# Gated linear attention rewritten by pairs of heads: half-array products, state updates on all partitions, PSUM banks of their own

## What is computed

```python
def gla_blocked(q, k, v, log_a, s0):
    bcum = jnp.cumsum(ac, axis=-2)            # per block of 64 (prompt) or 16 (streams) rows
    b_last = bcum[..., -1:, :]
    q_in, k_in = qc * jnp.exp(bcum), kc * jnp.exp(-bcum)
    att = jnp.where(causal, jnp.einsum('nbhik,nbhjk->nbhij', q_in, k_in), 0.0)
    o_intra = jnp.einsum('nbhij,nbhjv->nbhiv', att, vc)
    k_state = kc * jnp.exp(b_last - bcum)
    def step(s, inp):
        o = jnp.einsum('bhik,bhkv->bhiv', qi, s)
        s = at[..., None] * s + jnp.einsum('bhjk,bhjv->bhkv', ks, vi)
        return s, o
# then: rmsnorm(o, gla_g) * silu(ag)
```

## Time and profile before

| | us |
|---|---|
| median of 3 runs | 2823.79 (2822.34 to 2826.65) |
| the profiled execution, its own time | 2827.22 |
| its span, first to last instruction | 2825.4 |
| TensorE busy | 2717.4 (96%) |
| VectorE busy | 681.3 (24%) |
| ScalarE busy | 688.2 (24%) |
| GpSimd busy | 1054.1 (37%) |
| mean granted clock of TensorE | 0.968 of full speed |

### The profile page before, as it was taken

The page is one execution under the profiler, slowest core; times in us unless marked ns, Lnnn a source line. Parts: engine busy times, 40 slices in busy tenths (PEclk is TensorE's granted clock), DMA queues, the critical chain, the costliest instruction groups (busy, mean ns, idle before and its releaser), DMA issues.

```text
span 2825.4 us, 46758 instructions
## 1 busy us (share of the span) xinstructions
PE 2717.4 (96%) x19779; PEld 2580.6 (91%) x19779; DVE 681.3 (24%) x1442; ACT 688.2 (24%) x913; POOL 1054.1 (37%) x403
## 2 busy tenths in 40 slices
PE   7999999999889999999999999999988899999997
PEld 6999999998758999999999999999944489999997
DVE  4110113343443211112311011231133332110112
ACT  2221222220162221122222122221044532211221
POOL 3443444331043444344444334333223343443442
PEclk9999999998599999999999999999989999999998
DMA  3212211223062221221222222133699932222211
GB/s 134 75 60 85 79 58 63 90 75 128 11 237 104 67 76 63 90 75 59 78 78 68 78 82 70 57 108 97 227 358 372 366 120 75 74 67 82 74 62 65
DMA packets 57248, 302.96 MB, mean 107 GB/s; under 512 B 8337, under 2 KB 12194, under 8 KB 31026
## 3 DMA queue, kind: packets, MB, share of 16 engines
q1 hardware_dynamic: 57138, 301.38, 30.4%
HBM read 279.95 MB, written 21.41 MB: 107 GB/s over the span
## 4 chain that ended last, share of the span: by engine, by line
PE 91%; DMA 5%; DVE 2%; ACT 1%; POOL 1%; issue 0%; SPq 0%; DVEq 0%; ACTq 0%; POOLq 0%
PE ps L312 78%; PE ps L676 4%; DMA kv_ring<-in_fox_kc 2%; DMA kv_ring<-in_fox_vc 2%; PE ps L982 1%; PE ps L1016 1%; PE ps L941 1%; PE ps L956 1%; POOL w_lo L298 1%; PE ps L997 1%; PE ps L967 1%; PE ps L1271 0%; DVE xn_lo L413 0%; PE ps L1260 0%; PE ps L378 0%
## 5 line engine op out<-in xcount | busy, mean ns | idle before, releaser
L298 POOL TENSOR_TENSOR w_lo<-w_raw,w_hi 128x2048 fp32r<-128x2048 f32 (+2 forms) x185 | 791.7, 4280 | 687.6 <-ACT w_hi L293 679.2
L312 PE MATMUL ps<-xn_hi,w_hi 128*128 128x320 f32 x3616 | 830.1, 311 | 23.4 <-POOL w_lo L1649 11.0
L312 PE MATMUL ps<-xn_lo,w_hi 128*128 128x320 f32 x3616 | 827.1, 310 | 0.0
L312 PE MATMUL ps<-xn_hi,w_lo 128*128 128x320 f32 x3616 | 826.3, 310 | 0.0
L312 PEld LDWEIGHTS ps<-xn_hi,w_hi 128*128 128x128 f32 x3616 | 606.8, 189 | 25.8 <-POOL w_lo L1649 11.0
L312 PEld LDWEIGHTS ps<-xn_lo,w_hi 128*128 128x128 f32 x3616 | 607.9, 189 | 0.0
L312 PEld LDWEIGHTS ps<-xn_hi,w_lo 128*128 128x128 f32 x3616 | 607.3, 189 | 0.0
L293 ACT ACTIVATE w_hi<-w_raw 128x2048 fp32r<-128x2048 f32 (+2 forms) x185 | 326.6, 1766 | 535.0 <-PE ps L312 466.8
L565 POOL TENSOR_TENSOR h_lo<-prod,h_hi 128x640 f32 x88 | 139.0, 1580 | 716.2 <-ACT h_hi L518 716.2
L312 PE MATMUL ps<-h_hi,w_lo 128*128 128x320 f32 x1408 | 320.9, 309 | 0.0
L312 PE MATMUL ps<-h_hi,w_hi 128*128 128x320 f32 x1408 | 320.9, 309 | 0.0
(11 more groups left out here) (196 smaller groups left out, 1889.3 us busy)
## 6 DMA issues: line engine op xcount, KB each, us to landing
w_raw<-in_w_up SPq DMA_DIRECT2D x87, 1024.0 KB, 4.8
kv_ring<-in_fox_kc SPq DMA_DIRECT2D x32, 1024.0 KB, 13.1
kv_ring<-in_fox_vc SPq DMA_DIRECT2D x32, 1024.0 KB, 12.6
w_raw<-in_w_down_a SPq DMA_DIRECT2D x32, 768.0 KB, 4.2
w_raw<-in_w_in SPq DMA_DIRECT2D x24, 1024.0 KB, 4.9
w_raw<-in_w_down_b SPq DMA_DIRECT2D x32, 640.0 KB, 3.9
fox_s_s<-s_bias_dram SPq DMA_DIRECT2D x16, 576.0 KB, 9.8
kv_ring<-in_band_kc SPq DMA_DIRECT2D x8, 1024.0 KB, 6.2
```

Of the source, the lines that this page charges most:

```text
L298: nc.gpsimd.tensor_tensor(out=w_lo[:, slot, 0:cols], in0=w_raw[:, slot, 0:cols], in1=w_hi[:, slot, 0:cols].bitcast(F32), op=ALU.subtract). ...
L312: last = nc.tensor.matmul(ps[:, 2 * unit + half, 0:HALF], w_part[:, slot, w:w + P], a_part[:, k, half * HALF:(half + 1) * HALF], start=k = ...
```

## The change

Everything lies within the GLA.

- The two zero-filled copies of the queries are gone: one product of 128 partitions scales `qa`. Attention blocks and state products use the 64 rows of their head, in both operands.
- `head_psum` gives each head two banks of its own; `chunk_kv` each chunk a bank; `pair_att`, `pair_stats` and `stream_kv` place the rest. Products on rows 0-63 and on rows 64-127 that stand next to each other go to different banks. In the attention blocks two tiles share a pair of banks, so the masks wait for both.
- Chunk and stream products are now made by head, 64 columns of the array each, written to the partitions of that head. They hold no unused blocks. VectorE then copies and updates both heads of a pair in one instruction of 128 partitions. Chunk products no longer wait for the states, but (from the third chunk on) for the masks that free their banks.
- `pair_out` makes the outputs of two heads, the heads by turns. Squares have a tile for each head of a pair. The statistics, the inverse root (on ten columns) and the diagonals are made by pairs.
- The stream products come in two runs of four streams, with new places in the order: `pair_out(0)`, `pair_out(1)`, `pair_stat(0)`, two spreads, `pair_stat(1)`, four streams, two spreads, four streams.

```diff
-    qa1 = place("qa1", [P, 2, T], F32, at_e + tile_b)
     k_in = place("k_in", [P, 2, T], F32, at_e + 5 * tile_b)
     assert at_e + 7 * tile_b <= end
-    sq_head = place("sq_head", [P, T], F32, at_e)
+    sq_head = [place(f"sq_head{u}", [P, T], F32, at_e + u * tile_b) for u in range(2)]
...
-            pe.wait_ge(g_qk, 6)
+            pe.wait_ge(g_qk, 3)
...
+    def head_psum(h):
+        return flat((2, 4, 0, 6)[h], 2, T)
+    def pair_stats(pair):
+        return ps[:, (5, 7)[pair], 256:256 + 2 * TT]
+    def chunk_kv(c):
+        return ps[:, c, 0:256].rearrange("p (a v) -> p a v", a=2)
+    def pair_att(tt):
+        c0 = tt % 2 * 256
+        return ps[:, 2:8, c0:c0 + 256].rearrange("p (b r) (a c) -> p b r a c", r=2, a=2)[:, tt // 2, :, :, :]
+    def stream_kv(b):
+        return ps[:, 2 + b // 2, b % 2 * 256:b % 2 * 256 + 256].rearrange("p (a v) -> p a v", a=2)
...
-                last = nc.tensor.matmul(ps[:, 3 + tt, h * P:(h + 1) * P], k_in[:, h // 2, cols],
-                                        q_head[h % 2][:, h // 2, cols], start=True, stop=True)
+                last = nc.tensor.matmul(pair_att(tt)[:, h % 2, h // 2, :], k_in[head_rows[h], h // 2, cols],
+                                        qa[head_rows[h], h // 2, cols], start=True, stop=True)
             last.then_inc(g_att, 1)
         for c in range(SEQ // CHUNK):
             rows = slice(64 * (c % 2), 64 * (c % 2) + 64)
             if c >= 2:
...
+                pe.wait_ge(g_attm, min(c // 2 * 2, TT))
+            for h in range(H_A):
+                last = nc.tensor.matmul(chunk_kv(c)[head_rows[h], h // 2, :],
+                                        k_tok[rows, c // 2, h * DK:(h + 1) * DK],
+                                        va[rows, c // 2, h * P:(h + 1) * P], start=True, stop=True)
             last.then_inc(g_kv, 1)
         pe.wait_ge(g_attm, TT)
-        pe.wait_ge(g_s, 4 * (SEQ // CHUNK))
+        pe.wait_ge(g_s, 2 * (SEQ // CHUNK))
         pe.wait_ge(s_dec_loaded, 16)
...
+        def pair_out(pair):
+            heads = (2 * pair, 2 * pair + 1)
             for tt in range(TT):
-                nc.tensor.matmul(o[:, tt * P:(tt + 1) * P], va[:, tt, h * P:(h + 1) * P],
-                                 att[:, tt, h * P:(h + 1) * P], start=True, stop=False)
+                for h in heads:
+                    nc.tensor.matmul(head_psum(h)[:, tt * P:(tt + 1) * P], va[:, tt, h * P:(h + 1) * P],
+                                     att[:, tt, h * P:(h + 1) * P], start=True, stop=False)
                 if tt < TT - 1:
                     for c in (2 * tt, 2 * tt + 1):
                         if c:
                             cols = slice(c * CHUNK, (c + 1) * CHUNK)
-                            last = nc.tensor.matmul(o[:, cols], s_hist[:, c, pair, :], q[:, pair, cols],
-                                                    start=False, stop=c % 2 == 1)
+                            for h in heads:
+                                nc.tensor.matmul(head_psum(h)[:, cols], s_hist[head_rows[h], c, pair, :],
+                                                 qa[head_rows[h], pair, cols], start=False, stop=c % 2 == 1)
                 else:
                     for b in range(DEC_BATCH):
                         cols = slice(SEQ + b * DEC_SEQ, SEQ + (b + 1) * DEC_SEQ)
-                        last = nc.tensor.matmul(o[:, cols], s_dec[:, b, pair, :], q[:, pair, cols],
-                                                start=False, stop=b == DEC_BATCH - 1)
+                        for h in heads:
+                            last = nc.tensor.matmul(head_psum(h)[:, cols], s_dec[head_rows[h], b, pair, :],
+                                                    qa[head_rows[h], pair, cols], start=False,
+                                                    stop=b == DEC_BATCH - 1)
             last.then_inc(g_o, 1)
-        def head_stat(h):
-            pe.wait_ge(g_sq, h + 1)
+        def pair_stat(pair):
+            pe.wait_ge(g_oc, 2 * pair + 2)
+            for h in (2 * pair, 2 * pair + 1):
+                pe.wait_ge(g_sq, h + 1)
+                for tt in range(TT):
+                    last = nc.tensor.matmul(pair_stats(pair)[:, h % 2 * TT + tt:h % 2 * TT + tt + 1],
+                                            sq_head[h % 2][:, tt * P:(tt + 1) * P], mean_head[:, :], start=True,
+                                            stop=True)
+                last.then_inc(g_stat, 1)
+        def head_spread(h):
+            pe.wait_ge(diag_done, DIAG0["gla"] + TT * (h + 1))
             for tt in range(TT):
...
+                last = nc.tensor.matmul(head_psum(h)[:, tt * P:(tt + 1) * P], ones[:, :], diag_a[:, h % 2, tt, :],
                                         start=True, stop=True)
             last.then_inc(g_r, 1)
...
+        def streams_kv(first):
+            pe.wait_ge(g_kown, 1)
+            for b in range(first, first + 4):
+                for h in range(H_A):
+                    last = nc.tensor.matmul(stream_kv(b)[head_rows[h], h // 2, :], k_own[:, b, h * DK:(h + 1) * DK],
+                                            va[:, TT - 1, h * P:(h + 1) * P], start=True, stop=True)
+                last.then_inc(g_kv, 1)
+        pair_out(0)
+        pair_out(1)
+        pair_stat(0)
         head_spread(0)
-        head_stat(1)
-        head_out(3)
         head_spread(1)
...
+        pair_stat(1)
+        pe.wait_ge(g_on, 2)
+        streams_kv(0)
+        head_spread(2)
         head_spread(3)
+        pe.wait_ge(g_on, 4)
+        streams_kv(4)
...
-        for h in range(H_A):
-            act.wait_ge(g_o, h + 1)
-            if h == 2:
+        for pair in range(2):
+            heads = (2 * pair, 2 * pair + 1)
+            act.wait_ge(g_o, pair + 1)
+            if pair:
                 act.wait_ge(g_kown, 1)
...
+            for h in heads:
+                nc.scalar.activation(o_head[:, h, :], head_psum(h), ACT.Copy).then_inc(g_oc, 1)
+            for h in heads:
+                act.wait_ge(g_oc, h + 1)
+                if pair:
+                    act.wait_ge(g_stat, h - 1)
+                nc.scalar.activation(sq_head[h % 2][:, :], o_head[:, h, :], ACT.Square).then_inc(g_sq, 1)
...
-            nc.vector.tensor_tensor(out=qa1[64:P, :, :], in0=qa[64:P, :, :], in1=e_cum[64:P, :, :],
+            nc.vector.tensor_tensor(out=qa[:, :, :], in0=qa[:, :, :], in1=e_cum[:, :, :],
                                     op=ALU.mult).then_inc(g_qk, 1)
...
         for tt in range(TT):
...
+            dve.wait_ge(g_att, min(tt // 2 * 2 + 2, TT))
+            keep = (keep16 if tt == TT - 1 else keep64)[:, :].unsqueeze(1).unsqueeze(1).broadcast_to([P, 2, 2, P])
+            nc.vector.tensor_tensor(out=att[:, tt, :].rearrange("p (a r c) -> p r a c", a=2, r=2), in0=pair_att(tt),
+                                    in1=keep, op=ALU.mult).then_inc(g_attm, 1)
         for c in range(SEQ // CHUNK):
             dve.wait_ge(g_kv, c + 1)
             if c:
...
+                dve.wait_ge(g_s, 2 * c)
+            for pair in range(2):
+                kv = chunk_kv(c)[:, pair, :]
                 if c == 0:
-                    ins_ = nc.vector.tensor_copy(s_hist[rows, 1, pair, :], kv)
+                    ins_ = nc.vector.tensor_copy(s_hist[:, 1, pair, :], kv)
                 else:
                     col = (c + 1) * CHUNK - 1
-                    ins_ = nc.vector.scalar_tensor_tensor(out=s_hist[rows, c + 1, pair, :],
-                                                          in0=s_hist[rows, c, pair, :],
-                                                          scalar=e_cum[rows, pair, col:col + 1], in1=kv,
+                    ins_ = nc.vector.scalar_tensor_tensor(out=s_hist[:, c + 1, pair, :], in0=s_hist[:, c, pair, :],
+                                                          scalar=e_cum[:, pair, col:col + 1], in1=kv,
                                                           op0=ALU.mult, op1=ALU.add)
                 ins_.then_inc(g_s, 1)
...
...
+        def pair_norm(pair):
+            dve.wait_ge(g_stat, 2 * pair + 2)
+            rs_chain(dve, pair_stats(pair), pair * 2 * TT, 2 * TT, RS_NORM0["gla"] + pair * RS_OPS)
+            dve.wait_ge(rs_step, RS_NORM0["gla"] + (pair + 1) * RS_OPS)
+            if pair:
+                dve.wait_ge(g_r, 2)
+            for h in (2 * pair, 2 * pair + 1):
+                for tt in range(TT):
+                    nc.vector.tensor_scalar(out=diag_a[:, h % 2, tt, :], in0=ident[:, :],
+                                            scalar1=rs[1][:, h * TT + tt:h * TT + tt + 1], scalar2=None,
+                                            op0=ALU.mult).then_inc(diag_done, 1)
         def head_gated(h):
             dve.wait_ge(g_r, h + 1)
...
             else:
                 dve.wait_ge(g_sg, 1)
             nc.vector.scalar_tensor_tensor(out=o_tmp[:, :], in0=o_head[:, h, :], scalar=head_gain[:, 0:1],
```

(13 more changed lines are left out.)

88 lines of the change are left out of this document (4 added, 84 removed).

## The result

The changed kernel takes **2797.28 us** (median; 2795.59 to 2798.28, 4 runs), the kernel before 2825.22 us beside it (2822.34 to 2827.09, 4 runs): ratio 0.9901, 95% interval 0.9889 to 0.9913, so 24.6 to 31.4 us less. The forecast was 2797.5 us, its range 2786 to 2809.

The account below looks back on a forecast made before the run. Bound taken: the GLA stretch before the band attention, by VectorE's state chain, TensorE's per-record pace at low clock, then mutual waits. Attention starts at 752.9 instead of 779.25 us, -26.3 us: 2823.8 - 26.3 = 2797.5 us, range 2786 to 2809.

Parts of the forecast that it names:

- the new wait: GLA tail: TensorE waits 3.3 us for the first diagonals, with the first spread queued behind them.
- Scaled queries (1): Query scaling on VectorE, among projections: one 128-partition product replaces two products and two memsets; worth 0.
- Masks (2): VectorE's five attention-block masks run nearly back to back, ending near 686.0 instead of 686.6 us: -0.6 us.
- Chunk states (3): State chain with 128-partition updates, 0.83 us a chunk: outputs start at 692.6 instead of 700.75 us, -8.1 us.
- Outputs by pairs (4): GLA outputs on TensorE: 12.8 us a pair, 25.6 for both against 34.2 before, ten switches of 0.25 us a pair.
- The tail (5): GLA after the outputs, from 718.2 us: statistics, diagonals, spreads, stream products and gates, last gated product ending at 749.9 us.
- the granted clock stays 0.50 to the attention: Sign expected in the profile after: TensorE's clock stays low through the GLA until the band attention.
- The end (6): Cast, subtraction and state store as before; attention's first product at 752.9 instead of 779.25 us.
- the clock that comes back during the outputs: Rival: clock 1.00 from the second output pair on, 6.7 us for that pair, 14 us more gained, 2783.5 us; chance 14%.
- No overlap: Rival: state products within an output pair don't overlap, +6.0 us a pair, 2809.5 us; chance 9%.
- Attention at the low clock: Rival: band attention behind the GLA never regains its clock, up to 55 us added, some 2850 us; chance 3%.
- nothing gained: Rival: something else, say a transfer, holds the attention behind the GLA; time near 2822 us; chance 4%.

Follow-up runs that it names:

- updates_64_sorted: Changed kernel with VectorE's chunk-state copies and updates head by head on 64 partitions, heads ordered 0, 2, 1, 3: 2803.39 us, ratio 0.9922.
- before_states: Kernel before, plus only chunk products by head in 64 columns and VectorE's state copies and updates over 128 partitions: 2815.49 us, ratio 0.9973.
- outputs_grouped: Changed kernel with each pair's full-array output products all issued before its state products, two changes of shape a pair instead of ten: 2786.14 us, ratio 0.9874.
- heads_in_runs: Changed kernel with, within each tile, the even head's state products all before the odd head's instead of by turns: 2801.98 us, ratio 0.9923.
- stats_between: Changed kernel with the first pair's statistics issued within the second pair's outputs, before its third tile: 2795.31 us, ratio 0.9896.
- pool_held: Changed kernel with GpSimd's four GLA subtractions held until VectorE has made all twenty diagonals: 2794.89 us, ratio 0.989.
- clock_kept: Changed kernel plus five unused float32 products of 512 columns on TensorE during the chunk-state chain: 2791.75 us, ratio 0.9879.
- combined: Changed kernel with grouped outputs started during the state chain, first statistics behind the second pair's full-array products, GpSimd's subtractions held: 2773.67 us, ratio 0.9813.

## Why the prediction was right, point by point

The time came out within 0.3 us of the forecast, but that closeness is partly luck. The stage by itself gained 29.7 us where the sum had 26.3: the outputs started 1.8 us sooner than forecast, took 0.5 us longer, and the tail was 2.2 us shorter. Between the medians the gain was 27.9 us, and the median of before beside it lay 1.4 us above the 2823.8 from which the forecast was taken; the two differences of 1.6 and 1.4 us cancel. The profiled execution, forecast at 2800.9 us, took 2795.59. What was right is the order of the parts, the overlap and the new wait. By the steps, counted in the profiled executions:

- **Scaled queries (1): 0.** Nothing waited for them; the projections' end shows only the variation between runs. It wasn't tried by itself.
- **Masks (2): right.** They end 4.3 us after the first attention block; forecast 686.0 - 681.1 = 4.9, before 5.5. The masks start every 0.62 us, each taking 0.68, as they follow each other without a wait.
- **Chunk states (3): mechanism right, size off.** From masks to outputs 5.5 us, forecast 6.6; the start of the outputs comes 9.9 us sooner, forecast 8.1 (before 700.75 - 681.12 = 19.6, now 9.8). The mis-sized term is "each costs what a 64-partition one does: 1.49 / 4 = 0.37 us". The duration is indeed the same (0.34), but that 0.37 was the pitch of updates that change rows each time; wide ones follow every 0.265 us, and a chunk's boundary adds 0.18. So a chunk takes 0.71 us, below the forecast's 0.83 and outside its bounds of 0.75 and 1.1. `updates_64_sorted` shows it, and `before_states` shows that the wide updates alone carry this step.
- **Outputs by pairs (4): right.** 13.1 and 13.05 us, forecast 12.8 each. Ten switches at 0.25 us stand, by the records of the changed kernel (see `outputs_grouped`); the steps of two take 0.213 instead of 0.20. `heads_in_runs` shows the overlap. So the factor on 34.2 us of outputs is 1.31. The Trainium skill's table of theoretical speedups (TensorEngine Tiling (Array Packing), Theoretical Speedup) gives up to 2x. For the half-array products alone the trace comes near it: the attention blocks fell from 4.73 to 2.50 us at full clock, a pair's stream products from 2 x 3.23 to 3.53 us at the low one. For the outputs as a whole no run at the low clock shows it, since 20 of 80 records stay full-array (4.3 of 13.1 us now) and the switches take 2.5 us.
- **The tail (5): right in its shape, 2.2 us too long.** From the end of the outputs to the band's first product 32.5 us, forecast 34.7. The new wait before the first spread is 3.41 us (forecast 3.3), as `stats_between` confirms by removing it. Two terms were too small: the statistics 4.37 instead of 3.88, and the meeting of VectorE and GpSimd, which happened twice for 2.6 us instead of once for 1.0 (`pool_held`). So the path was another in the middle: the second inverse root doesn't wait for the statistics, as forecast, but for the lengthened gate, and starts at 730.52 us, 1.1 us after they ended. The clock, which the forecast had wrong (below), and the last eight updates, 2.2 us instead of 8 x 0.37 = 3.0, more than made up for them.
- **The clock: wrong.** The sign "the granted clock stays 0.50 to the attention" failed: it was 1.00 from about 726 to 730 and again from 740 us. The second pair's statistics took 2.29 instead of 3.9 us, the last stream products 2.20 instead of 3.7.
- **The end (6): right.** Cast, subtraction, store (3.85 us) and start of the band as before, and an unchanged attention.

Of the rivals, the clock that comes back during the outputs did not occur here, but was nearer than its 14% made it look: an edit of the order brings it. Its price was right: 6.7 us for a pair at full clock, measured 7.0 in `clock_kept`. The argument against it, 44.8 us of unbroken work at 0.50, was true of that order alone. The rule weighed there (the Trainium skill, TensorE: Matmul & The Clock Gate, the two states), that sustained work releases the throttle, is borne out by `outputs_grouped` and the tail, and contradicted by 26 us of by-turns work. No overlap: out by `heads_in_runs`. Attention at the low clock, and nothing gained: neither came.

## What to carry to other kernels

Between two phases at the low clock, look at the order of the products before their number: a run of full-array products first, small half-array ones behind it, brought 11 us, as against some 8 us that halving the outputs' array rows had brought; and filling an idle stretch ahead of a matrix phase kept the clock into it, with unused products (`clock_kept`) as with the phase's own first ones (`combined`). Size a chain of dependent small instructions by the pitch of such instructions on the same rows, not by that of neighbours that change rows. When a VectorE instruction with two SBUF inputs is on the path, look at what GpSimd runs beside it: holding GpSimd back took 2.5 us off this stage.
